# Decoder trunk on one core: expert token lists built once a layer, gates carried by the gathered rows, shared expert's down projection moved ahead of the expert loop

## The reference

```
scores = sigmoid(x @ w_router)                      # 272 x 64
sel    = scores + router_bias                       # 8 groups of 8 experts, best 4 groups kept
top_idx = top_k(sel in the kept groups, 8)          # 8 experts for each token
gates  = scores[top_idx] / sum * 2.5
routed = sum over the chosen e: gates[e] * (silu(x @ w_gate[e]) * (x @ w_up[e])) @ w_down[e]
shared = (silu(x @ ws_gate) * (x @ ws_up)) @ ws_down
h      = layer_norm(alpha * h + routed + shared)
```

## Time and profile before

| | |
|---|---|
| median of 3 runs | 1687.0 us (1684.89 to 1687.05) |
| the profiled execution | 1687.35 us, its span 1685.6 us |
| PE busy | 1611.8 us, 96% of the span |
| PEld / DVE / ACT / POOL busy | 902.6 / 397.7 / 267.4 / 173.6 us |
| DMA | 470.73 MB, mean 279 GB/s |
| mean granted clock | 0.956 |

### The profile page before, as it was taken

How to read it: one execution, slowest core, us unless ns; L and a number is a source line. 1 busy time by engine, 2 the same in 40 slices (tenths; PEclk the granted TensorE clock), 3 DMA queues, 4 the chain that set the end, 5 groups by cost and what they waited for, 6 DMA issues and landing times. The chain is left out here.

```text
span 1685.6 us, 25764 instructions
## 1 busy us (share of the span) xinstructions
PE 1611.8 (96%) x9774; PEld 902.6 (54%) x9774; DVE 397.7 (24%) x1246; ACT 267.4 (16%) x608; POOL 173.6 (10%) x192
## 2 busy tenths in 40 slices
PE   8999989999999999999699998999999999999994
PEld 6776475454454454454376754745445445445452
DVE  1521431212111212112316223311211111211213
ACT  1243101111110111111112421011111101111111
POOL 1021210000000000000212023000000000000002
PEclk9997989999999999999889969899999999999997
DMA  9421428999997999997282214299999979999950
GB/s 352 176 101 51 156 85 350 384 362 383 360 382 309 369 362 385 364 383 286 101 288 85 102 60 183 97 363 365 381 365 381 377 312 352 382 366 380 386 219 26
DMA packets 97562, 470.73 MB, mean 279 GB/s; under 512 B 9328, under 2 KB 13552, under 8 KB 64096
## 3 DMA queue, kind: packets, MB, share of 16 engines
q1 hardware_dynamic: 85040, 442.19, 66.2%
q0 software_dynamic: 11856, 25.55, 4.4%
q10 hardware_dynamic: 608, 2.23, 0.3%
HBM read 484.48 MB, written 3.28 MB: 289 GB/s over the span
## 5 line engine op out<-in xcount | busy, mean ns | idle before, releaser
L535 PE MATMUL bank<-ring,region 128*64 128x256 f32 x4096 | 480.9, 380 | 1.9 <-issue 1.9
L535 PEld LDWEIGHTS bank<-ring,region 128*64 128x64 f32 x4096 | 297.9, 137 | 169.7 <-issue 38.0
L503 PE MATMUL bank<-region 128*128 128x512 f32 x528 | 276.0, 606 | 0.0
L565 PE MATMUL bank<-ring,region 128*64 128x512 f32 x1024 | 248.0, 605 | 0.0
L1476 POOL DMA_INDIRECT region<-h_rows,rank_i x68 | 67.7, 996 | 1113.5 <-DVE rank_i L1165 1088.3
L620 PE MATMUL bank<-hT,ring 128*128 128x272 f32 (+1 forms) x704 | 173.7, 406 | 2.9 <-issue 2.0
L939 ACT ACTIVATE region<-bank 128x512 f32<-128x512 f32 x128 | 76.4, 597 | 493.1 <-PE bank L565 493.1
L620 PEld LDWEIGHTS bank<-hT,ring 128*128 128x128 f32 (+1 forms) x704 | 135.1, 195 | 35.7 <-issue 4.5
L565 PEld LDWEIGHTS bank<-ring,region 128*64 128x64 f32 x1024 | 62.1, 136 | 148.9 <-issue 100.3
L503 PEld LDWEIGHTS bank<-region 128*128 128x128 f32 x528 | 80.2, 191 | 55.6 <-issue 55.6
L1164 DVE COPY region<-bank 128x2 f32<-128x2 f32 x68 | 10.8, 159 | 405.5 <-PE bank L477 405.5
(11 more groups left out here) (169 smaller groups left out, 1087.5 us busy)
## 6 DMA issues: line engine op xcount, KB each, us to landing
ring<-in_w_down_dram SPq DMA_DIRECT2D x64, 2048.0 KB, 7.6
ring<-in_w_gate_dram SPq DMA_DIRECT2D x64, 2048.0 KB, 9.7
ring<-in_w_up_dram SPq DMA_DIRECT2D x64, 2048.0 KB, 10.4
ring<-in_w_in_dram SPq DMA_DIRECT2D x8, 2048.0 KB, 14.1
ring<-in_w_o_dram SPq DMA_DIRECT2D x4, 2048.0 KB, 13.5
ring<-in_w_in_dram SPq DMA_DIRECT2D x2, 1824.0 KB, 9.4
ln_par<-in_ln_g_dram POOLq DMA_DIRECT2D x4, 512.0 KB, 5.4
ln_par<-in_ln_b_dram POOLq DMA_DIRECT2D x4, 512.0 KB, 7.3
```

Of the source, the lines that this page charges most:

```text
L503: last = mm(bank[SUM_BANKS[n][half]][0:w, :], selg[:, u, t0:t0 + w], y_sb[:, u, half * 512:(half + 1) * 512], start=opens, stop=stop, skip ...
L535: last = mm(bank[5][64 * e:64 * e + 64, part * F:(part + 1) * F], xgT[:, u, kk, 64 * e:64 * e + 64], w[:, e, kk, :], start=(kk == 0), stop ...
L565: last = mm(bank[6][64 * e:64 * e + 64, :], mo["h2"][:, j * 128 + 64 * e:j * 128 + 64 * e + 64], w[:, e, j, half * 512:(half + 1) * 512], ...
```

## The change

- **Lists.** `chosen` is transposed on PE to experts x tokens (three transposes, into bank 5). DVE makes from it a row for each of the 64 experts that holds 4096 - t for each of its tokens t and zeros elsewhere (`left`, one instruction). Then `make_lists` takes the eight largest values of every row eight times over: `max`, then `match_replace` by zero, 64 partitions x 272 elements, each waiting for the one before it. That gives `list`, the first 64 tokens of each expert. Two matmuls on PE (`turn_lists`) bring it to 128 slots x 32 pairs, and DVE writes all indices (`rank_i`, 128 x 32) and token numbers (`idf`) in two instructions (`read_lists`). The rank matmuls, `route`, `select` and `slot_rows` are gone.
- **Gates.** A row of h in DRAM is 1088 numbers long in place of 1024: the last 64 are the token's gates, written by SP once a layer. The gather brings them along, and DVE picks the pair's two (`read_gate`, L1165 of the changed kernel, one instruction on 128 x 2 with a sum).
- **Gathers** are 32 in place of 34 a layer, written out one by one; each waits until the buffer's rows are transposed and its gates read.
- **Shared down** stands between `turn_lists` and the loop, opens the PSUM sums, and is the only work that is there. The first pair has no scatter, the last has no transposes of a further pair. So pairs 0, 1 and 30, 31 are written out and 28 run in the hardware loop.
- **Layers** are written out (`for l in range(DEPTH)`) in place of a hardware loop, on all engines.

Cut to its core:

```diff
-        h_rows = nc.dram_tensor("h_rows", [T, D], F32, kind="Internal").ap()
+        h_rows = nc.dram_tensor("h_rows", [T, ROW], F32, kind="Internal").ap()
...
 (SP)
+                sp.wait_ge(gates_ready, l + 1)
+                sp.dma_start(h_rows[0:META, D:ROW], gates[0:META, 0, :]).then_inc(gates_stored, 16)
...
 (PE)
-            def slot_rows(g, q, before, evac):
-
-                pe.wait_ge(before, evac)
-                pe.wait_ge(sel_ready, g * 34 + q + 1)
+            def turn_lists(g):
+
+                hold_here(pe, list_step, g * (CAP // 4) + CAP // 4)
+                own = k["ident"][0:64, 0:64].rearrange("p (q e) -> p e q", e=2)
                 for e in range(2):
-                    for n, (t0, w) in enumerate(CHUNKS):
-                        last = mm(bank[7][64 * e:64 * e + 64, 0:2], sel[0:w, n, e, :], pb[0:w, n, e, 0:2],
-                                  start=(n == 0), stop=(n == 2))
-                last.then_inc(slot_row_done, 1)
+                    last = mm(bank[7][64 * e:64 * e + 64, 0:PAIRS], mo["list"][0:64, :], own[:, e, :], start=True, stop=True)
+                last.then_inc(list_turned, 1)
...
                             if part == 1:
-                                slot_rows(g, p + 2, ht_ready, g * 32 + p)
                                 pe.wait_ge(slot_in[base + 1], arrived[1])
...
+                pe.wait_ge(ws_down_in, l * 16 + 16)
+                pe.wait_ge(shared_ready, l * 2 + 1)
+                shared_down(0, 0)
+                shared_down(1, 0)
+                pe.wait_ge(shared_ready, l * 2 + 2)
+                shared_down(2, 0)
+                for n in range(3):
+                    last = shared_down(n, 1)
+                last.then_inc(scattered, 1)
                 round_(l, 0, False)
...
 (DVE)
+                def read_gate(q, u):
+                    dve.scalar_tensor_tensor(mo["gpair"], xg[:, u, bass.ds(D + q * 2, 2)], 1.0, k["half"], ALU.mult, ALU.mult,
+                                             accum_out=mo["gsel"][:, u:u + 1]).then_inc(gate_read, 1)
...
+            def make_lists(g):
+
+                for j in range(CAP // 8):
+                    dve.max(mo["list"][0:64, 8 * j:8 * j + 8], mo["left"][0:64, :]).then_inc(list_step, 1)
+                    hold_here(dve, list_step, g * (CAP // 4) + 2 * j + 1)
+                    dve.match_replace(mo["left"][0:64, :], mo["list"][0:64, 8 * j:8 * j + 8], mo["left"][0:64, :], 0.0)\
+                        .then_inc(list_step, 1)
+                    hold_here(dve, list_step, g * (CAP // 4) + 2 * j + 2)
+
+            def read_lists(g):
+
+                dve.wait_ge(list_turned, g + 1)
+                dve.tensor_scalar(rank_i[:, :], bank[7][:, 0:PAIRS], -1.0, FAR, ALU.mult, ALU.add).then_inc(ids_ready, 1)
+                dve.tensor_scalar(mo["idf"], bank[7][:, 0:PAIRS], -1.0, None, ALU.mult).then_inc(idf_ready, 1)
+                dve.wait_ge(idf_ready, g + 1)
...
 (POOL)
+                hold_here(pool, ids_ready, g + 1)
+                for q in range(PAIRS):
+                    u = q % 2
+                    if q >= 2:
+                        hold_here(pool, xtb_done, g * 32 + q - 1)
+                        hold_here(pool, gate_read, g * 32 + q - 1)
                     pool.indirect_dma_start(out=xg[:, u, :], out_offset=None, in_=h_rows,
```

More of the change, by code:

```diff
@@ L83, in shape_constants @@
     p = np.arange(128)
-    c = {"ident": np.eye(128), "before": p[:, None] < p[None, :], "ones": np.ones((128, 128))}
+    c = {"ident": np.eye(128), "ones": np.ones((128, 128))}
     half = R_QK // 2
@@ L596, in round_ @@
                 pe.reg_add(rounds_run, rounds_run, 1)
-            with pe.Fori(0, DEPTH) as l:
+            for l in range(DEPTH):
                 pe.wait_ge(hT_act, l * 6 + 3)
@@ L874, in _, with shared_down @@
                                       start=(kk == 0), stop=(kk == KC - 1))
-                            if j == 1 and (part, kk) in ((0, KC - 1), (1, 3)):
-                                slot_rows(l * ROUNDS, part, slot_row_ready, l * (ROUNDS * 34) + part)
                     last.then_inc(shared_done, 1)
-                pe.wait_ge(rank_ready, l + 1)
                 pe.wait_ge(score_ready, l * 2 + 2)
+                turn_lists(l * ROUNDS)
+                def shared_down(n, j):
+                    t0, w = CHUNKS[n]
+                    for q in range(4 if n == 0 else 2):
+                        if n == 0:
+                            o, c0, cols = bank[SUM_BANKS[0][0]][32 * q:32 * q + w, 0:256], q * 256, 256
+                        else:
+                            o, c0, cols = bank[SUM_BANKS[n][q]][0:w, :], q * 512, 512
+                        last = mm(o, hsT[:, j, t0:t0 + w], wsd[:, j, c0:c0 + cols], start=(j == 0), stop=False,
+                                  skip_group_check=True)
+                    return last
+                pe.wait_ge(ws_down_in, l * 16 + 16)
[7 more added lines that the diff above has]
+                last.then_inc(scattered, 1)
                 round_(l, 0, False)
@@ L940, in round_ @@
                                 .then_inc(y_ready, 1)
-            with act.Fori(0, DEPTH) as l:
+                turned(0, 0)
+                two_pairs(0, first=True)
+                with act.Fori(1, PAIRS // 2 - 1) as i:
+                    two_pairs(i)
+                two_pairs(PAIRS // 2 - 1, final=True)
+            for l in range(DEPTH):
                 def proj(b):
@@ L1202, in round_ @@
                         dve.tensor_tensor(mo["h"], mo["ha"], bank[5][:, F:2 * F], ALU.mult).then_inc(h_ready, 1)
-                        turned(p + 1, 1 - u)
+                        if not (final and u == 1):
+                            turned(p + 1, 1 - u)
+                            read_gate(p + 1, 1 - u)
                         dve.wait_ge(ht_done, g * 32 + p + 1)
                         dve.tensor_copy(mo["h2"], bank[7][:, 0:F]).then_inc(ht_ready, 1)
-            with dve.Fori(0, DEPTH) as l:
+                with dve.Fori(0, PAIRS // 2 - 1) as i:
+                    two_pairs(i)
+                two_pairs(PAIRS // 2 - 1, final=True)
+            def make_lists(g):
[10 more added lines that the diff above has]
+                dve.wait_ge(idf_ready, g + 1)
+            for l in range(DEPTH):
                 steps[0] = 0
```

268 lines of the change are left out of this document (108 added, 160 removed).

## The result

The changed kernel takes 1618.17 us (median of 4 runs, 1616.06 to 1621.19) against 1685.95 us for the kernel before, run beside it (median of 4): a ratio of 0.9601, 95% interval 0.9585 to 0.9617. Forecast: 1625 us, range 1614 to 1644. The profiled execution took 1618.31 us, with a span of 1616.5.

A forecast was written before the change was run, and what follows sets the result against it. PE was taken to bound the expert loops. Slot rows -64.6, MoE start +7.4, loop ends -4.0 and written-out layers -1.0 sum to -62.2 us, from 1687.35 to 1625.2, stated as 1625; 8-in-10 range 1614 to 1644 us.

The forecast's parts named there:

- the slot rows are its own time: Expert loops: the slot rows cost 1.01 us of PE's time a pair, so removing them over 64 pairs gives -64.6 us.
- DMA would follow: Expert loops: at 418 GB/s DMA needs 15.8 us of a 16.53 us pair, so PE doesn't notice; cost 0.
- The two DMA rivals: Expert loops: 390 GB/s in a full pair gives 1650 us, 7%; 376 GB/s as the limit gives 1693 us, 3%.
- Gathers, read_gate, gates to DRAM, GpSimd's tables: 0: Row gathers, DVE's gate reading, SP's gate writes and dropped table zeroing: each 0 us; read_gate at worst +13 us.
- The start of a MoE stage: From the rank matmuls to the first transposes: +1.2 us, with the clock +3.7 us a layer, +7.4 us in all.
- Half clock at shared down: Near the start of shared down: PE's clock drops to half after idling, costing 2.5 us a layer, bounds 0 and 8.5.
- The rival of dear lists: List rounds: held waits cost 0.58 us each and the clock stays low, +25.8 us, 1651 us; chance 10%.
- The first pair: First expert pair of each layer: loses its scatter of zeros, 4 us of which about 1 remains as gain.
- Last pair and layer edge: Last pair saves 1.0 us a layer on unused transposes; the written-out layer edge saves 1.0 us; -3.0 together.
- Fetching in the loop: Rival: PE fetches instructions at each loop turn in the expert loops, +36 us, 1661 us; chance 4%.
- the up phase took nothing back: Rival: the up phase takes back part of the slot rows' gain, up to +20 us, 1645 us; chance 6%.

The follow-up runs named there:

- a shorter pair: Changed kernel with the four 512-column routed-sum matmuls of each pair cut to 256 columns: layer 0 pairs took 15.73 us, 3641.41 us in all.

## Why the prediction was right

- **PE bounds the loop, and the slot rows are its own time.** Right, and shown by putting them back. The term was mis-sized by 0.09 us a pair, 5.8 us in all: I took the up phase as equal to the gate phase, but one stream of 64 records is shorter than two of 32.
- **DMA would follow.** Right: 399 GB/s with no wait for `ring`, and 415 with a shorter pair. The two DMA rivals (390 GB/s in a full pair; 376 as the limit) fall. The 221 GB/s at a pair's start show the pause being used up, as the working had it. One slip that moves nothing: the longer rows add 128 x 64 x 4 bytes = 0.03 MB a pair, not 0.02.
- **Gathers, read_gate, gates to DRAM, GpSimd's tables: 0.** Right as far as the trace tells: PE has 0.01 us of idle time in a pair.
- **The start of a MoE stage.** The steps held: a round of 1.21 us where the working had 1.02 + 2 x 0.12 = 1.26; shared down starts 13.99 us after the transposes of the choice, 14.55 forecast; idle time of 3.0 to 3.4 us and 1.6 us. Half clock at shared down cost 10.49 - 8.45 = 2.0 us; 2.5 forecast. The rival of dear lists falls with the round's time.
- **The first pair: the step that failed.** I gave it -1.0 us, and its work has just that: where no half-clock stretch falls into it, it takes 15.37 us, 1.07 less than a steady pair. But in the changed kernel a second half-clock stretch falls into it, in both layers, and it takes 18.25 and 16.66. The working charged the clock once a layer, for shared down, and put it at nothing for the first pair, which has no scatter to cover its trips (0.69 and 0.83 us idle just ahead of it, 0.69, 0.88, 0.52 and 0.69 in it). These trips alone don't explain the stretch: with plain waits, and with the earlier choice, they are the same and the pair runs at 2.4 GHz. The waits further ahead bear on it too; how stays open. That is 4.0 us, on the wrong side of a term of -2.0.
- **Last pair and layer edge.** -4.2 for -3.0. The edge was worth 1.2 us against the kernel before (0.83 for 2.00) and 1.5 against the changed one with hardware loops (2.36), no more than the total's scatter.
- **The other rivals.** Fetching in the loop would have shown as idle PE; the up phase took nothing back, rather the reverse.

The total came out 6.9 us below the forecast, nearly all of it the 5.8 us of the slot rows. That the other terms' errors cancel (4.0 us too much hope for the first pair; 1.7, 1.2 and 1.9 us too little for the start, the ends and the stage ahead) is luck. The 1.9 us ahead of the rank matmuls, where nothing on the path was changed, are of the size by which that stage differs between the kernels run here: their transposes of the choice start at 231.81, 232.84, 232.36 and 230.21 us in four with the same work up to there. Much of that spread goes with the clock. Of the seven kernels with this place unmoved, four have 6.8 us less at 1.2 GHz between 55 and 205 us, and get there at 229.9 to 230.4 though their first 80 records take 1.7 us more; the other three get there at 231.8 to 232.8. The kernel before (232.99) and the changed one have stretches of equal length there, so their own difference stays unexplained.

## What to carry to other kernels

When an engine is busy without a gap and its suppliers wait for it, tiny instructions on it are worth their full time: here 12 of them were 4% of the kernel. Before removing work that stands between a trip to another engine and its return, ask what it covers: here leaving out four pieces of the scatter made the kernel slower, since the clock fell in each pair once the trips stood uncovered. After a change that adds a wait, look at what the wait does to the clock further on, and put independent work of the same engine into the gap; here half of a projection, the order of two VectorE steps, a slightly earlier transpose and plain waits were worth another 1.1% together (1600.08 against 1618.17 us).

## What the runs showed of the hardware

- With waits of 3.0 + 1.6 us on PE around the transposes of the lists, the clock fell to 1.2 GHz for 6.8 us within the first wait and for another 6.8 us in the first pair (6.8 and 3.4 in layer 1). With 1.4 + 1.7 or 1.7 + 1.7 us one stretch of 6.8 us was left, with 0.2 + 1.6 or 0.6 + 1.6 us two of 3.4, with 0.25 + 0.55 us none at shared down. A shorter wait did not always give a shorter stretch.
- The same idle times of PE in the first pair (0.69, 0.88, 0.52 and 0.69 us) went with 6.8, 3.4 or 0 us at 1.2 GHz in it: 18.25, 16.66 and 15.37 us for the same work.
- The same code ahead of the router took 2.5 us less in layer 1 of an execution that had 6.8 us less at 1.2 GHz there (219.81 for 222.34 us).
- A loop can fall in step with the clock's drops: a period of 15.6 us became 17.27 and then 17.07, with a stretch of 3.4 us at 1.2 GHz in each, for as long as the loop ran.
- PE idle for 0.7 us in each pair of 15.73 us kept 2.4 GHz; idle for 2.1 us did not.
- DMA reached 415 GB/s as a mean over 225 us, where the kernel before had 376 over the same window.
- A wait that holds VectorE costs 0.11 us more than a plain one.
